# Compressed attention scores: each head pair against its own group's 32 key columns, in one bank, collected by one addition

## What is computed

```python
s_c = jnp.einsum('bgrqd,bgnd->bgrqn', qc, kc).astype(jnp.float32) - slopes * dist_c
p_c = masked_softmax(s_c, dist_c >= 0)
o_c = jnp.einsum('bgrqn,bgnd->bgrqd', p_c.astype(vc.dtype), vc)
...
o = gc[..., 0:1] * o_c + gc[..., 1:2] * o_s + gc[..., 2:3] * o_w
```

## Time and profile before

| What | Value |
|---|---|
| Median of 3 runs | 1077.8 us (1074.75 to 1078.85) |
| The profiled execution, its own time | 1077.36 us |
| Its span, first to last instruction | 1075.6 us |
| Mean granted TensorE clock | 0.990 |
| TensorE busy | 1022.8 us, 95% |
| DVE busy | 766.0 us, 71% |
| ACT busy | 701.2 us, 65% |

### The profile page before, as it was taken

How to read it: one execution, slowest core, us unless ns; L and a number is a source line. 1 busy time by engine, 2 the same in 40 slices (tenths; PEclk the granted TensorE clock), 3 DMA queues, 4 the chain that set the end, 5 groups by cost and what they waited for, 6 DMA issues and landing times.

```text
span 1075.6 us, 17447 instructions
## 1 busy us (share of the span) xinstructions
PE 1022.8 (95%) x6136; PEld 853.4 (79%) x6136; DVE 766.0 (71%) x1347; ACT 701.2 (65%) x1201; POOL 96.8 (9%) x181
## 2 busy tenths in 40 slices
PE   7988899999998999899999999999989999999998
PEld 6876789999997877787788778767878688877866
DVE  5686557666666657778668878877777668888876
ACT  6665545444445536575588989857676489899855
POOL 9017000000000100000420000000000330000000
PEclk9999999999999999999999999999999899999999
DMA  9871027666654555004439999854424429999951
GB/s 295 288 254 40 1 96 237 186 185 181 188 176 166 160 189 198 1 2 157 176 131 317 350 335 332 302 192 148 128 78 157 176 88 319 339 337 338 329 169 40
DMA packets 106156, 209.25 MB, mean 195 GB/s; under 512 B 7736, under 2 KB 51744, under 8 KB 105824
## 3 DMA queue, kind: packets, MB, share of 16 engines
q1 hardware_dynamic: 103584, 204.04, 55.7%
q0 software_dynamic: 2064, 3.25, 1.1%
q10 hardware_dynamic: 432, 0.99, 0.2%
HBM read 207.19 MB, written 1.06 MB: 194 GB/s over the span
## 4 chain that ended last, share of the span: by engine, by line
PE 85%; DVE 7%; ACT 4%; issue 2%; DMA 1%; ACTq 0%; SPq 0%; POOL 0%; DVEq 0%; POOLq 0%
PE bank L882 23%; PE bank L1639 17%; PE bank L1658 11%; PE bank L1312 8%; PE bank L1322 8%; PE bank L997 4%; PE bank L986 2%; PE bank L976 2%; PE bank L786 2%; PE bank L2139 1%; PE bank L1680 1%; PE bank L1469 1%; PE bank L1507 1%; PE bank L1650 1%; DMA expert_w<-in_moe_w_up 1%
## 5 line engine op out<-in xcount | busy, mean ns | idle before, releaser
L882 PE MATMUL bank<-weight_parts,x_high 128*128 128x512 f32 (+2 forms) x768 | 223.2, 375 | 8.6 <-ACT x_high L850 2.6
L1639 PE MATMUL bank<-expert_high,block_high 128*128 128x256 f32 x560 | 183.8, 328 | 3.4 <-ACT block_low L1587 2.4
L1567 DVE TENSOR_TENSOR expert_low<-expert_w,expert_high 128x1024 fp32r<-128x1024 f32 x140 | 164.7, 1219 | 9.9 <-ACT expert_high L1560 9.5
L882 PEld LDWEIGHTS bank<-weight_parts,x_high 128*128 128x128 f32 x768 | 139.1, 188 | 35.6 <-ACT x_high L850 7.0
L1639 PE MATMUL bank<-expert_high,block_low 128*128 128x256 f32 x560 | 158.2, 282 | 0.0
L1639 PE MATMUL bank<-expert_low,block_high 128*128 128x256 f32 x560 | 158.0, 282 | 0.0
L903 DVE TENSOR_TENSOR weight_parts<-ring,weight_parts 128x1024 fp32r<-128x1024 f32 (+3 forms) x112 | 121.1, 1104 | 51.2 <-ACT weight_parts L900 50.7
L900 ACT CAST weight_parts<-ring 128x1024 fp32r<-128x1024 f32 (+3 forms) x112 | 104.4, 958 | 75.6 <-PE bank L882 55.4
L1560 ACT CAST expert_high<-expert_w 128x1024 fp32r<-128x1024 f32 x140 | 140.2, 1053 | 19.3 <-DMA expert_w<-in_moe_w_up 18.9
L882 PE MATMUL bank<-weight_parts,x_low 128*128 128x512 f32 (+2 forms) x384 | 143.1, 373 | 0.0
L1658 PE MATMUL bank<-expert_w,junk 128*128 128x512 f32 x280 | 131.3, 592 | 0.0
(11 more groups left out here) (356 smaller groups left out, 1693.2 us busy)
## 6 DMA issues: line engine op xcount, KB each, us to landing
expert_w<-in_moe_w_gate SPq DMA_DIRECT2D x70, 512.0 KB, 5.7
expert_w<-in_moe_w_up SPq DMA_DIRECT2D x70, 512.0 KB, 7.4
expert_w<-in_moe_w_down SPq DMA_DIRECT2D x70, 512.0 KB, 5.5
ring<-in_w_ff SPq DMA_DIRECT2D x64, 512.0 KB, 3.9
ring<-in_w_in SPq DMA_DIRECT2D x16, 512.0 KB, 8.5
ring<-in_a_w_in SPq DMA_DIRECT2D x16, 512.0 KB, 6.6
ring<-in_ple_w_gate SPq DMA_DIRECT2D x16, 512.0 KB, 5.7
ring<-in_w_o SPq DMA_DIRECT2D x8, 512.0 KB, 4.4
```

Of the source, the lines that this page charges most:

```text
L882: mm = nc.tensor.matmul(bank[:, j["m"] % 4, 0:n], j["operand"][x][:, 2 * c + kk, at[0]:at[1]], weight_parts[:, number % PAIRS, w, kk * n:( ...
L1567: nc.vector.tensor_tensor(half_of(expert_low[:, b % DEPTH, 0:2048], j), half_of(expert_w[:, b % DEPTH, 0:2048], j), half_of(expert_high[:, ...
L1639: mm = nc.tensor.matmul(bank[:, 4 + b % 2, 0:256].rearrange("p (q n) -> p q n", q=2), x[:, b % 2, k, :], w[:, k], start=k == 0 and n == 0, ...
```

## The change

The loops over groups and pairs become one loop over tiles and the 8 chunks. Each product takes as its moving side only the 16 columns of the chunk's own group in both halves of kcT, 32 columns in all, and writes 32 columns of bank 4. 2 x 8 x 32 columns fill this bank. One signal follows the last product. One addition over 128x512 elements takes all scores, and those who waited for four signals wait for one.

```diff
         if compressed:
-            pe.wait_ge(c_scored, KV_HEADS)
+            pe.wait_ge(c_scored, 1)
         turn_probs(first)
...
     def pe_compressed_scores(pe):
-        for g in range(KV_HEADS):
-            for t in range(TILES):
-                for pair in range(2):
-                    at = t * 256 + pair * P
-                    mm = nc.tensor.matmul(bank[:, 4 + g, at:at + P], nqT[:, 2 * g + pair, t * P:(t + 1) * P],
-                                          kcT[:, :, :].rearrange("p x n -> p (x n)"), start=True, stop=True)
-            mm.then_inc(c_scores, 1)
+        for t in range(TILES):
+            for c in range(KB):
+                at = t * 256 + c * 32
+                mm = nc.tensor.matmul(bank[:, 4, at:at + 32].rearrange("p (x n) -> p x n", x=2),
+                                      nqT[:, c, t * P:(t + 1) * P],
+                                      kcT[:, :, CMP_PAD * (c // 2):CMP_PAD * (c // 2 + 1)], start=True, stop=True)
+        mm.then_inc(c_scores, 1)
...
     def dve_take_compressed_scores(dve):
-        for g in range(KV_HEADS):
-            dve.wait_ge(c_scores, g + 1)
-            nc.vector.tensor_tensor(cl[:, :, 4 * g:4 * g + 4, :],
-                                    bank[:, 4 + g, :].rearrange("p (t r n) -> p t r n", t=TILES, r=4)[
-                                        :, :, :, CMP_PAD * g:CMP_PAD * (g + 1)],
-                                    const("cmp_dist").rearrange("p (t n) -> p t n", t=2).unsqueeze(2).to_broadcast(
-                                        [P, TILES, 4, CMP_PAD]), ALU.add).then_inc(c_scored, 1)
+        dve.wait_ge(c_scores, 1)
+        nc.vector.tensor_tensor(cl[:, :, :, :], bank[:, 4, :].rearrange("p (t h n) -> p t h n", t=TILES, h=HEADS),
+                                const("cmp_dist").rearrange("p (t n) -> p t n", t=TILES).unsqueeze(2).to_broadcast(
+                                    [P, TILES, HEADS, CMP_PAD]), ALU.add).then_inc(c_scored, 1)
 
     def dve_shift_compressed(dve):
-        dve.wait_ge(c_scored, KV_HEADS)
+        dve.wait_ge(c_scored, 1)
```

## The result

| | Before | After |
|---|---|---|
| Median | 1075.32 us, 15 runs (1074.01 to 1078.85) | 1080.45 us, 15 runs (1078.03 to 1082.17) |
| Profiled execution, its span | 1077.36, 1075.6 us | 1080.82, 1079.0 us |
| Mean granted TensorE clock in it | 0.990 | 0.985 |

The ratio of after to before is 1.0037, with a 95% interval of 1.0026 to 1.0049: the change costs about 4 us. That is clear of the measurement's noise but under the 0.5% set as the bound, and 1080.45 lies in the stated range. The medians themselves lie 5.1 us apart; the ratio, which uses all 15 runs of each, says 4. Single executions of a few kernels took 1458 us or more; they are in no ratio, and the only profile of before_again is one of them.

A forecast was written before the change was run, and what follows sets the result against it. TensorE was taken as the bound, 85% of the chain lying on it. Matmuls 0, additions 0, signals 0 and clock 1.0 + 0.7 + 0.8 = 2.5, on the profiled 1077.36, gave 1079.9 us; range 1075.0 to 1083.0.

The forecast's parts named there:

- Matmuls: term 0: Compressed scores L1146 on TensorE: 32 pairs keep their pace of 0.111 us at 32 columns, the weight load setting it; 0.
- Rival (2): At L1146 the pace of pairs follows the columns, 0.057 us instead of 0.111; 1.6 us gained, 1075.8 us; chance 0.05.
- Additions, signals, banks: terms 0: DVE's one later addition fits its idle time before L1081; fewer signals and unwritten banks let nothing start earlier; 0 each.
- the 0.26 us of cover: DVE's idle time before the first L1081, expected to be left over after the addition's 0.40 us later end.
- The clock: TensorE's half clock from 428.7 us goes on past 432.1; 1.0 + 0.7 + 0.8 = 2.5 us lost.
- Rival (1): After the narrow products at L1146 the low clock ends as before, all terms 0; 1077.4 us; chance 0.31.
- rival (3): The half clock holds through 445.7 us over the whole compressed stage; 5.8 us lost, 1083.2 us; chance 0.07.
- (4): The low stretch at 445.8 us falls away by the shift; 1076.1 us; chance 0.07.
- part is lost in DVE's own work: 0.8: Last part of the clock term: next batch's L976 up to 0.9 us longer, partly absorbed by DVE; 0.8 us.
- the case I gave 0.50: The forecast itself: one or two further low stretches of TensorE's clock after 432.1 us, 2.5 us in all; chance 0.50.
- the upper end of its clock term: TensorE's clock low until 442.2 us, its 8.70 us of work from 432.1 doubled, ending at 449.5; 4.3 us lost.

The follow-up runs named there:

- before_again: The kernel before, run once more with nothing changed; ratio to before 1.0007.
- one_bank_wide: The changed kernel, but each product's own 32 columns repeated to 128 (the last three 96, 64, 32); one bank, signal and addition kept; ratio to before 1.0001.
- narrow_four_banks: The kernel before with only the products narrowed to 32 columns; four banks, four signals and four additions stay; ratio to before 1.0038.
- wide_late_adds: The kernel before with 128 columns and four banks, but all four additions wait for the last product; ratio to before 0.9999.
- change_again: The changed kernel, run once more with nothing else changed; ratio to before 1.0034.
- routing_wide: The kernel before with the first layer's routing logits (L1454) multiplied with 128 columns instead of 36, the second layer kept at 36; ratio to before 1.0017.
- half_wide: The kernel before with 64 columns a product instead of 128, four banks and four additions kept; ratio to before 1.0045.

## Why the prediction was right, and where it was off

**Matmuls: term 0.** Right. 0.213 at the half clock, and 3.49 against 3.57 us for 32 pairs at the full one. The gap formula of the Trainium skill ("TensorE: Matmul & The Clock Gate", Back-to-back issue gap) is, by the words of that section, for an isolated matmul; it does not fit these pairs of a full float32 weight load and a matmul, whose pace is the same with 32 columns as with 128. Rival (2) falls.

**Additions, signals, banks: terms 0.** Right, and shown by one_bank_wide, narrow_four_banks and wide_late_adds. The idle time before L1081 stayed with L976, and the 0.26 us of cover were measured as 0.25.

**The clock.** Its direction was right: 0.50 past 432. Rival (1), that gapless narrow work keeps the clock, falls in three profiles (the change, change_again, narrow_four_banks) and in the second layer of routing_wide, and the mean clock over all executions agrees. The Trainium skill's advice (same page, Why this matters for your kernels) to keep TensorE continuously busy is not enough in this case: TensorE was busy for 12.89 of the 13.50 us of the low stretch. Rivals (3) and (4) did not come about either: the clock was back at 442.2, not past 445.7, and the later low stretch of 445.8 did not fall away but came at 449.0.

**The size of the clock term was too small**, and the term that failed is the last: "part is lost in DVE's own work: 0.8". Part by part, from the profiles of before and after: the products 6.16 against 5.44, 0.7 more (put at 1.0). From the first product to the first L1081 7.87 against 6.42, 1.45 more (put at 1.7). From there to the third batch of scores 12.72 against 10.92, 1.8 more (put at 0.8). The forecast was one or two further low stretches like that of 3.4 us; the half clock lasted until 442.2, three further. So what came was not the case I gave 0.50, but the upper end of its clock term, priced at 4.3; it measured 3.25.

That price had a slip in it, and rival (3)'s of 5.8 has the same: it doubled all of TensorE's work up to the time at which the clock returns, though work that has slid behind that time runs at the full clock. Up to the L986 that releases DVE's L1090, TensorE does 59 matmuls behind the products in both kernels. After the change they take from 433.68 to 444.04, 10.36 us instead of 7.84, and the last nineteen of them already ran at the full clock. From L1090 on nothing more is lost. The chain of before has there

```profile
441.06 0.56 DVE probT L1090
```

and reaches the third batch 4.12 us later, at 445.18; after the change it is 4.11 us, from 444.07 to 448.18. DVE's own compressed work sets the pace there in both.

**The number.** 1079.9 was built on one execution of before at 1077.36. Over 15 runs before stands at 1075.32, after at 1080.45. So the level was 2.0 us too high and the step between the medians, 5.1 instead of 2.5, was 2.6 too small (1.5 too small by the ratio's 4 us); the two errors nearly cancel, and that the number came so close is luck. The profiled execution of before had a low stretch of 3.4 us in the products; profiles of kernels with the same products have none. The forecast said that one trace cannot show this, and then used the one trace as if it were typical. Against an execution without the low stretch the change loses 20.59 - 15.72 = 4.9 us, against the profiled one 3.25; the measured 4 us, 0.37%, lie between.

**What stays open.** Where in the program the half clock of half_wide lies in most executions, and how often before has a low stretch in its products, would need more profiles than were taken. So would the question what lets the clock return: the half clock outlasted the narrow products by 8.5 us, and six wide matmuls among them did not bring it back at once.

## What to carry to other kernels

With full 128x128 float32 weights, cutting the moving side under 128 columns buys nothing here: look at the time from pair to pair at another width in the same trace before counting columns. A run of narrow matmuls (32, 36 or 64 columns here) can bring the clock to half or leave it there, for 3.4 to 13.5 us in these traces, busy as TensorE may be, so columns that nobody needs may be free, or better. Judge this by the mean clock of many executions, not by one profile: a low stretch was in the wide products of one profile and not in those of others. A low stretch of the clock costs by where it lies: moved off work that hides it, it can turn a saving into a loss.

## What the runs showed that was not expected

Wide matmuls of no use ahead of the narrow products, some 1.3 us of them at the full clock, made the changed kernel some 0.5% faster (its ratio to before went from 1.0037 to 0.999), while the same matmuls among the narrow products made it slower (1.0062). And half of the columns, 64, was no better than a quarter: 1.0045 against 1.0038.
